# Summing the squares of two rmsnorms: running total on VectorE, or a matmul per row block on TensorE

## The chip, the cores and the metric

The kernel runs on one core of a Trainium2 chip, as one program. The metric is the device time of one execution in microseconds (us). Before the change the median of three timed runs is 3715.22 us (3713.12 to 3716.41).

## The reference

The reference is one decoder layer for a 512-token prompt and 8 decode tokens together (520 columns in the kernel). What matters here are two of its rmsnorms: `h2 = rmsnorm(x, g_ffn)` after the output projection, and the final `rmsnorm(xp, g_final)`.

```python
def rmsnorm(x, g):
    y = xf * lax.rsqrt(jnp.mean(xf * xf, axis=-1, keepdims=True) + EPS) * g
...
    x = x + mix @ lp['w_out']
    h2 = rmsnorm(x, lp['g_ffn'])
    x = x + peer(h2, ...)
...
y_prompt = rmsnorm(xp, g_final)
```

The mean runs over the 2048 model channels of a token, so each norm needs, per token, the sum of 2048 squares.

## The kernel before

The activations lie channel-first: `xt` is 128 partitions x 16 blocks (`KT`) x 520 tokens. One block `xt[:, k, :]` holds 128 channels of all tokens. A sum over channels is therefore a sum over 16 blocks and then over 128 partitions. The sum over partitions is a matmul with a 128x128 matrix of ones, in f32, in two column halves of 264 and 256 (`HALVES`), because a PSUM bank takes 512 columns.

The program has five stages with a barrier of all engines between them: `stage_a` (input projection), `stage_m` (attention and state space), `stage_d` (GLU and output projection), `stage_e` (PEER scores and the expert inputs), `stage_f` (the expert outputs and the final norm). Each engine runs its own instructions in the order in which they are written and is tied to the others by semaphores. Nothing is scheduled by a planner.

All weights come as 324 units of 1 MB. Each goes through SP's queue (DMA to `raw`), ScalarE (`split_hi`, the rounded upper part `wh`), GpSimd (`split_lo`, the rest `wl`), and then TensorE, with three fp32r matmuls per tile (`wh` with the upper and the lower part of the moving data, `wl` with the upper part). Two buffers alternate.

In `stage_d` the output projection has 16 units of 96 matmuls, one unit for each block of `xt`. The first has a loop of its own (L1204 to L1206), the others go through `unit_matmuls` (L138 to L140). After a unit, VectorE adds the result to `xt` (L1270), ScalarE squares that block into one of two slots of `sq` (L1158) and stores it, and VectorE adds the square to a running total (L1276). After the last unit TensorE multiplies the total by the ones (L1215). The next stage begins with a square root of the result (L1357).

In `stage_f` a group (`g`, 32 of them) has four units (`n`), and a unit has four tiles (`d`) of 12 matmuls (L1806 to L1808). Each tile belongs to one block of `xt`, and VectorE adds it there (L1878). Only in the last group do the blocks become final. From its second unit on ScalarE squares them (`square`, L1764), four to a unit, into four slots of `sq`. VectorE adds them to a total in `rs` (`add_square`, L1848 and L1851), two after each tile of the units 2 and 3. Then come the matmul with ones (L1822), the square root (L1789), the reciprocal (L1890) and 16 multiplications (L1894), each followed by its store.

ScalarE's order in the last group is: the split of the weights for unit 3, which waits for the tiles of unit 1, and only behind it the squares 0 to 3.

Of the kernel before, what the change touches and what calls it, by code (L numbers as in the profile page):

```python
# [12 lines left out]
ALU = mybir.AluOpType  # L13
# [6 lines left out]
KT = D // P  # L20
NS, NT = 8, 512
T = NS + NT
HALVES = ((0, 264), (264, 256))
H = 8
# [1058 lines left out]
def stage_d(nc, m, ins, outs):  # L1083

    at, sem = m.at, m.sem
# [3 lines left out]
    sq = at("sq2", [P, 4, T]); stg = at("stg", [P, 2, 2, T]); rs = at("head_rs", [H, T]); bgl = at("bgl", [P, 8]); gsub = at("gsub", [P, 2])  # L1089
    to_row = at("to_row", [P, H, H]); from_row = at("from_row", [H, H, P])  # L1090
    gh, gl = m.gh, m.gl
    total = sq[:, 2, :]
    S = {n: sem("d_" + n) for n in "const_in x_in row_ready head_squared head_summed head_root root_inverse head_spread head_scaled gain_ready heads_hi heads_lo glu_tile glu_kept sigmoid_ready mixed mixed_hi mixed_lo squares_ready squares_added residual_added".split()}
    with nc.Block() as block:
        @block.sync
        def _(sp):
# [25 lines left out]
        @block.scalar  # L1122
        def _(act):
            act.wait_ge(S["const_in"], 32)
            for n in range(N_GLU):
                u = U_GLU + n
                for j, (t, hf) in enumerate(GLU_TILES):
                    act.wait_ge(S["glu_tile"], 4 * n + j + 1)
                    if n >= 2 and hf == 0:
                        act.wait_ge(S["mixed"], 2 * (n - 2) + t + 1)  # L1130
                    c0, w = HALVES[hf]
                    act.activation(stg[:, n % 2, t, c0:c0 + w], m.acc[:, t, hf, 0:w], ACT.Sigmoid, bias=bgl[:, 2 * n + t:2 * n + t + 1]).then_inc(S["glu_kept"], 1)
                if n == N_GLU - 1:
                    act.wait_ge(S["glu_kept"], 4 * N_GLU)
                    act.sem_inc(m.acc_free, N_GLU)
                split_hi(m, act, u + 2, n % 2, (u + 2) // 2)
                if n == 0:
                    act.wait_ge(S["head_summed"], H)
                    for hf, (c0, w) in enumerate(HALVES):
                        act.activation(rs[:, c0:c0 + w], m.aux[0:H, hf, 0:w], ACT.Sqrt, bias=m.eps[0:H, 0:1], scale=1.0 / P).then_inc(S["head_root"], 1)  # L1140
                if n == N_GLU - 1:
                    for h in HEADS_SPLIT[n]:
                        act.wait_ge(S["head_scaled"], 2 * h + 2)
                        act.activation(m.hh[:, h, :], ot[:, h, :], ACT.Copy).then_inc(S["heads_hi"], 1)
                for t in range(2):
                    act.wait_ge(S["mixed"], 2 * n + t + 1)
                    act.activation(m.hh[:, 8 + 2 * n + t, :], yg[:, 2 * n + t, :], ACT.Copy).then_inc(S["mixed_hi"], 1)
                if n < N_GLU - 1:
                    for h in HEADS_SPLIT[n]:
                        act.wait_ge(S["head_scaled"], 2 * h + 2)  # L1150
                        act.activation(m.hh[:, h, :], ot[:, h, :], ACT.Copy).then_inc(S["heads_hi"], 1)
            with act.Fori(0, N_OUT // 2) as i:
                for s in range(2):
                    split_hi(m, act, i * 2 + (U_OUT + s + 2), s, i + (U_OUT // 2 + 1))

                    act.wait_ge(S["residual_added"], i * 2 + (s + 1))
                    act.wait_ge(S["squares_added"], i * 2 + (s + 1))
                    act.activation(sq[:, s, :], m.xt[:, ds(i * 2 + s, 1), :].rearrange("p a n -> p (a n)"), ACT.Square).then_inc(S["squares_ready"], 1)  # L1158
                    act.dma_start(m.x2[:, ds(i * 2 + s, 1), :].rearrange("p a n -> p (a n)"), m.xt[:, ds(i * 2 + s, 1), :].rearrange("p a n -> p (a n)")).then_inc(m.x2_stored, 16)

        @block.tensor
        def _(pe):
# [43 lines left out]
                    mm = pe.matmul(o, m.wl[0][:, k, :], m.hh[:, k, c0:c0 + w], start=False, stop=(k == KT - 1))  # L1206
            mm.then_inc(m.mm_done, 1)

            unit_matmuls(m, pe, U_OUT + 1, 1, m.hh, m.hl, 1)
            with pe.Fori(0, N_OUT // 2 - 1) as i:  # L1210
                for s in range(2):
                    unit_matmuls(m, pe, i * 2 + (U_OUT + s + 2), s, m.hh, m.hl, s)
            pe.wait_ge(S["squares_added"], KT + 2)
            for h, (c0, n) in enumerate(HALVES):
                pe.matmul(m.aux[:, h, 0:n], m.ones[:, :], total[:, c0:c0 + n], start=True, stop=True)  # L1215

        @block.vector
        def _(dve):
            dve.memset(to_row[:, :, :], 0.0).then_inc(S["row_ready"], 1)
            dve.tensor_copy(from_row[:, :, :], m.ident[0:H, 0:H].unsqueeze(2).broadcast_to([H, H, P])).then_inc(S["row_ready"], 1)  # L1220
            dve.wait_ge(S["row_ready"], 2)
# [38 lines left out]
                    for h in HEADS_SPLIT[n]:  # L1260
                        head_low(h)
            dve.wait_ge(S["x_in"], 16)
            dve.wait_ge(S["head_summed"], H)
            dve.memset(total, 0.0).then_inc(S["squares_added"], 2)
            with dve.Fori(0, N_OUT // 2) as i:
                for s in range(2):
                    dve.wait_ge(m.mm_done, i * 2 + (U_OUT + s + 3))
                    for hf, (c0, n) in enumerate(HALVES):
                        x = m.xt[:, ds(i * 2 + s, 1), c0:c0 + n].rearrange("p a n -> p (a n)")
                        x = dve.tensor_tensor(x, x, m.acc[:, s, hf, 0:n], ALU.add)  # L1270
                    x.then_inc(S["residual_added"], 1)
                    dve.wait_ge(S["residual_added"], i * 2 + (s + 1))
                    dve.sem_inc(m.acc_free, 1)
                    dve.wait_ge(S["squares_ready"], i * 2 + (s + 1))
                    dve.wait_ge(S["squares_added"], i * 2 + (s + 2))
                    dve.tensor_tensor(total, total, sq[:, s, :], ALU.add).then_inc(S["squares_added"], 1)  # L1276

TK = 16
HK = H * TK
# [8 lines left out]
GRP, NG = 4, 32  # L1288
# [399 lines left out]
def stage_f(nc, m, ins, outs):  # L1688
# [10 lines left out]
    sq = at("sq3", [P, 4, T]); rs = at("rs3", [P, T])  # L1699
    vg = [at(f"vg{j}", [P, D]) for j in range(GW)]  # L1700
    y_tok = m.aux[:, :, :].rearrange("p a n -> p (a n)")
    S = {n: sem("g_" + n) for n in "x_in ain0 ain1 gin0 gin1 weighed first_weighed weighed_hi first_hi weighed_lo first_lo sum_added tile_done rows_added y_kept y_turned squares_ready squares_added squares_summed root_ready out_ready out_stored".split()}
    ain, gin = [S["ain0"], S["ain1"]], [S["gin0"], S["gin1"]]
    vg_in = [sem(f"g_vgin{j}") for j in range(GW)]
    with nc.Block() as block:
# [42 lines left out]
        def _(act):  # L1748
# [10 lines left out]

            def square(k):  # L1760
                if k >= 4:
                    act.wait_ge(S["squares_added"], k - 3)
                act.wait_ge(S["sum_added"], 4 + 16 * (NG - 1) + k + 1)
                act.activation(sq[:, k % 4, :], m.xt[:, k, :], ACT.Square).then_inc(S["squares_ready"], 1)  # L1764

# [18 lines left out]
            turn(NG // 2 - 1, True)  # L1784
            for k in range(KT - 4, KT):
                square(k)
            act.wait_ge(S["squares_summed"], 1)
            for h, (c0, n) in enumerate(HALVES):
                act.activation(rs[:, c0:c0 + n], m.aux[:, h, 0:n], ACT.Sqrt, bias=m.eps[:, 0:1], scale=1.0 / D).then_inc(S["root_ready"], 1)  # L1789

        @block.tensor
        def _(pe):
            def turn(i, last):
                for gg in range(2):
                    g = i * 2 + gg
                    pe.wait_ge(S["weighed_lo"], g + 1)
                    for n in range(4):
# [12 lines left out]
                        if last and gg == 0 and n == 3:  # L1810
                            pe.wait_ge(S["y_kept"], 1)
                            for k in range(KT):
                                mm = pe.transpose(m.aux[:, k // 4, P * (k % 4):P * (k % 4) + P], y_sb[:, P * k:P * k + P], m.ident[:, :])
                                if k % 4 == 3:
                                    mm.then_inc(S["y_turned"], 1)

            with pe.Fori(0, NG // 2 - 1) as i:
                turn(i, False)
            turn(NG // 2 - 1, True)
            pe.wait_ge(S["squares_added"], KT)  # L1820
            for h, (c0, n) in enumerate(HALVES):
                mm = pe.matmul(m.aux[:, h, 0:n], m.ones[:, :], rs[:, c0:c0 + n], start=True, stop=True)  # L1822
            mm.then_inc(S["squares_summed"], 1)

        @block.vector
        def _(dve):
# [11 lines left out]
            def add_row(k):  # L1838
# [3 lines left out]
                else:  # L1842
                    dve.wait_ge(S["rows_added"], k)
                    dve.scalar_tensor_tensor(y_tok, vg[k % GW][:, :], m.w0[:, k:k + 1], y_tok, ALU.mult, ALU.add).then_inc(S["rows_added"], 1)  # L1844
            def add_square(k):
                dve.wait_ge(S["squares_ready"], k + 1)
                if k == 0:
                    dve.tensor_copy(rs[:, :], sq[:, 0, :]).then_inc(S["squares_added"], 1)  # L1848
                else:
                    dve.wait_ge(S["squares_added"], k)  # L1850
                    dve.tensor_tensor(rs[:, :], rs[:, :], sq[:, k % 4, :], ALU.add).then_inc(S["squares_added"], 1)  # L1851

            dve.wait_ge(ain[0], 16)
            dve.wait_ge(gin[0], 16)
            for e in range(GRP):
# [10 lines left out]
            for g in range(NG):  # L1866
                for n in range(4):
# [6 lines left out]
                    for d in range(4):  # L1874
# [4 lines left out]
                        if d == 1:  # L1879
                            for k in range(sums_by(j), sums_by(j + 1)):  # L1880
                                add_row(k)
                        if g == NG - 1 and n >= 2:
                            for k in range(8 * n + 2 * d - 16, min(8 * n + 2 * d - 14, KT)):
                                add_square(k)
                    if n == 1 and g + 1 < NG:
                        weigh(g + 1)
                    if n == 2 and g + 1 < NG:
# [2 lines left out]
            dve.reciprocal(rs[:, :], rs[:, :]).then_inc(S["tile_done"], 1)  # L1890
            dve.wait_ge(S["tile_done"], 16 * NG + 1)
            for k in range(KT):
                dve.wait_ge(S["squares_summed"], 1)
                dve.scalar_tensor_tensor(m.xt[:, k, :], m.xt[:, k, :], m.gains[:, 2, k:k + 1], rs[:, :], ALU.mult, ALU.mult).then_inc(S["out_ready"], 1)  # L1894


# [105 lines left out]
```

## Time and profile before

| | |
|---|---|
| timed runs, median | 3715.22 us |
| the profiled execution's own time | 3715.22 us |
| its span in the trace | 3713.4 us |
| TensorE busy | 3500.0 us (94%) |
| VectorE busy | 2172.1 us (58%) |
| ScalarE busy | 1066.3 us (29%) |
| GpSimd busy | 1911.3 us (51%) |
| mean granted TensorE clock | 0.978 |

The span is what the trace covers, and the rest of the execution (1.8 us) lies around it. PE is TensorE, PEld its weight loads, DVE VectorE, ACT ScalarE, POOL GpSimd. A matmul's row in the trace is longer than the distance to the next one, because matmuls overlap: throughput is read from the distance between starts. One f32 matmul appears as two rows, so a pair of them over both halves is "x4".

### The profile page before, as it was taken

The page shows a single profiled execution, that of the slowest core. Times are in us where ns is not written, and L with a number is a line of the kernel's source. Part 1 is how long each engine was busy: PE and PEld are TensorE (multiplying, and loading weights), DVE is VectorE, ACT ScalarE, POOL GpSimd, SP SyncE. Part 2 cuts the span into 40 slices and gives each one's busy share as a digit, 9 for nine tenths or more (in the row PEclk, how much of TensorE's full clock was granted, in tenths as well). Part 3 has the DMA queues.
Part 4 walks back from the last instruction along what each step waited for, and adds up shares of the span by engine and source line. Part 5 has one row for each costly group of instructions (what it writes and reads, how often), then busy time and mean ns, then how long its engine had stood idle before and what let it go on. Part 6 is the DMA issues. An engine that isn't in the chain of part 4 may idle for free. (4 is left out here: it accounts for less than half of the span.)

```text
span 3713.4 us, 57544 instructions
## 1 busy us (share of the span) xinstructions
PE 3500.0 (94%) x22728; PEld 3311.5 (89%) x22728; DVE 2172.1 (58%) x3937; ACT 1066.3 (29%) x1164; POOL 1911.3 (51%) x725
## 2 busy tenths in 40 slices
PE   8999987789998999999999999997999999999997
PEld 7978854447997999999999999997999999999997
DVE  6843224225444999964454444543677777777775
ACT  4111132243223232333333333332222222222222
POOL 3423206002334445665666666654766676767673
PEclk9999989999998999999999999998999999999998
DMA  4497978572322235767777677767778878778783
GB/s 158 159 356 296 356 275 301 180 238 108 123 101 81 79 113 194 285 264 273 274 294 278 266 279 297 280 267 275 298 278 301 298 286 301 288 296 301 291 295 129
DMA packets 257541, 910.77 MB, mean 245 GB/s; under 512 B 98353, under 2 KB 131634, under 8 KB 179378
## 3 DMA queue, kind: packets, MB, share of 16 engines
q1 hardware_dynamic: 170642, 558.22, 42.2%
q0 software_dynamic: 36864, 268.45, 17.5%
q10 hardware_dynamic: 49888, 82.24, 6.3%
q8 instruction: 81, 1.33, 0.1%
q14 instruction: 66, 0.54, 0.0%
HBM read 828.34 MB, written 78.12 MB: 244 GB/s over the span
## 5 line engine op out<-in xcount | busy, mean ns | idle before, releaser
L123 POOL TENSOR_TENSOR wl<-raw,wh 128x2048 fp32r<-128x2048 f32 x322 | 1515.8, 4708 | 1378.4 <-ACT wh L119 1378.4
L119 ACT ACTIVATE wh<-raw 128x2048 fp32r<-128x2048 f32 x324 | 620.4, 1915 | 2061.9 <-PE acc L1477 713.2
L1806 PE MATMUL acc<-vh,wh 128*128 128x392 f32 x2048 | 703.5, 344 | 42.1 <-DVE xt L1878 21.3
L1475 PE MATMUL acc<-hh,wh 128*128 128x392 f32 x2048 | 709.8, 347 | 7.1 <-POOL wl L123 7.1
L1476 PE MATMUL acc<-hl,wh 128*128 128x392 f32 x2048 | 698.5, 341 | 0.0
L1807 PE MATMUL acc<-vl,wh 128*128 128x392 f32 x2048 | 696.7, 340 | 0.0
L1477 PE MATMUL acc<-hh,wl 128*128 128x392 f32 x2048 | 696.0, 340 | 0.0
L1808 PE MATMUL acc<-vh,wl 128*128 128x392 f32 x2048 | 695.7, 340 | 0.0
L138 PE MATMUL acc<-hh,wh 128*128 128x256 f32 (+1 forms) x1952 | 555.8, 285 | 12.7 <-POOL wl L123 6.2
L139 PE MATMUL acc<-hl,wh 128*128 128x256 f32 (+1 forms) x1952 | 553.0, 283 | 0.0
L140 PE MATMUL acc<-hh,wl 128*128 128x256 f32 (+1 forms) x1952 | 551.4, 282 | 0.0
L1631 DVE SCALAR_TENSOR_TENSOR ug<-ug,aux 128x2048 f32<-128x2048 f32 x128 | 292.6, 2287 | 301.6 <-DMA ug<-expert_u,idx 300.9
L1806 PEld LDWEIGHTS acc<-vh,wh 128*128 128x128 f32 x2048 | 385.2, 188 | 53.2 <-DVE xt L1878 31.4
L1878 DVE TENSOR_TENSOR xt<-xt,acc 128x392 f32<-128x392 f32 x512 | 274.7, 557 | 220.6 <-PE acc L1808 214.2
L138 PEld LDWEIGHTS acc<-hh,wh 128*128 128x128 f32 x1952 | 369.3, 189 | 29.8 <-issue 19.0
L1475 PEld LDWEIGHTS acc<-hh,wh 128*128 128x128 f32 x2048 | 385.2, 188 | 7.4 <-ACT ast L1401 7.4
L1476 PEld LDWEIGHTS acc<-hl,wh 128*128 128x128 f32 x2048 | 385.4, 188 | 0.0
L1808 PEld LDWEIGHTS acc<-vh,wl 128*128 128x128 f32 x2048 | 385.3, 188 | 0.0
L1807 PEld LDWEIGHTS acc<-vl,wh 128*128 128x128 f32 x2048 | 385.3, 188 | 0.0
L1477 PEld LDWEIGHTS acc<-hh,wl 128*128 128x128 f32 x2048 | 385.2, 188 | 0.0
L139 PEld LDWEIGHTS acc<-hl,wh 128*128 128x128 f32 x1952 | 369.2, 189 | 0.0
L140 PEld LDWEIGHTS acc<-hh,wl 128*128 128x128 f32 x1952 | 369.0, 189 | 0.0
(335 smaller groups left out, 3954.1 us busy)
## 6 DMA issues: line engine op xcount, KB each, us to landing
raw<-units SPq DMA_DIRECT2D x324, 1024.0 KB, 4.8
kr<-cache_k SPq DMA_DIRECT2D x128, 512.0 KB, 6.8
vr<-cache_v SPq DMA_DIRECT2D x128, 512.0 KB, 6.2
expert_acts<-ast ACTq DMA_DIRECT2D x128, 196.0 KB
expert_gates<-gs ACTq DMA_DIRECT2D x14, 1792.0 KB, 6.3
a<-expert_acts SPq DMA_DIRECT2D x32, 784.0 KB
g<-expert_gates SPq DMA_DIRECT2D x32, 784.0 KB
output_steps<-qo ACTq DMA_DIRECT2D x16, 288.0 KB, 8.2
```

The source lines that it names most:

```text
L119: act.activation(m.wh[s][:, :, :], m.raw[s][:, :, :], ACT.Copy).then_inc(m.hi_done, 1)
L123: pool.tensor_tensor(m.wl[s][:, :, :], m.raw[s][:, :, :], m.wh[s][:, :, :].bitcast(F32), ALU.subtract).then_inc(m.lo_done, 1)
L138: pe.matmul(o, m.wh[s][:, k, :], rhs_hi[:, k, c0:c0 + n], start=(k == k_range[0]), stop=False)
L139: pe.matmul(o, m.wh[s][:, k, :], rhs_lo[:, k, c0:c0 + n], start=False, stop=False)
L140: mm = pe.matmul(o, m.wl[s][:, k, :], rhs_hi[:, k, c0:c0 + n], start=False, stop=(k == k_range[-1]))
L1475: pe.matmul(o, m.wh[s][:, k, :], m.hh[:, k, NA:T], start=(k == 0), stop=False)
L1476: pe.matmul(o, m.wh[s][:, k, :], m.hl[:, k, NA:T], start=False, stop=False)
L1477: mm = pe.matmul(o, m.wl[s][:, k, :], m.hh[:, k, NA:T], start=False, stop=(k == KT - 1))
L1631: dve.scalar_tensor_tensor(ug[k % GW][:, :], ug[k % GW][:, :], 1.0, m.aux[:, :, :].rearrange("p a n -> p (a n)"), ALU.mult, ALU.mult, accu ...
L1806: pe.matmul(o, m.wh[s][:, 4 * e + d, :], vh[gg][:, e, :], start=(e == 0), stop=False)
L1807: pe.matmul(o, m.wh[s][:, 4 * e + d, :], vl[gg][:, e, :], start=False, stop=False)
L1808: mm = pe.matmul(o, m.wl[s][:, 4 * e + d, :], vh[gg][:, e, :], start=False, stop=(e == GRP - 1))
```

## The change

In both stages the running total on VectorE is taken out. TensorE multiplies each block's square by the ones itself and lets PSUM accumulate over the 16 blocks (`start` at the first, `stop` at the last). The semaphore `squares_added`, which freed a slot of `sq` for ScalarE, becomes `squares_summed`, raised by TensorE after each pair.

```diff
 (stage_d, ScalarE)
-                    act.wait_ge(S["squares_added"], i * 2 + (s + 1))
+                    act.wait_ge(S["squares_summed"], i * 2 + (s + 1))
 (stage_d, TensorE)
+            def add_squares(s, count, first=False, last=False):
+
+                pe.wait_ge(S["squares_ready"], count)
+                for h, (c0, n) in enumerate(HALVES):
+                    mm = pe.matmul(m.aux[:, h, 0:n], m.ones[:, :], sq[:, s, c0:c0 + n], start=first, stop=last, skip_group_check=True)
+                mm.then_inc(S["squares_summed"], 1)
+
             unit_matmuls(m, pe, U_OUT + 1, 1, m.hh, m.hl, 1)
+            add_squares(0, 1, first=True)
             with pe.Fori(0, N_OUT // 2 - 1) as i:
                 for s in range(2):
                     unit_matmuls(m, pe, i * 2 + (U_OUT + s + 2), s, m.hh, m.hl, s)
-            pe.wait_ge(S["squares_added"], KT + 2)
-            for h, (c0, n) in enumerate(HALVES):
-                pe.matmul(m.aux[:, h, 0:n], m.ones[:, :], total[:, c0:c0 + n], start=True, stop=True)
+                    add_squares(1 - s, i * 2 + (s + 2))
+            add_squares(1, KT, last=True)
 (stage_d, VectorE)
+            dve.sem_inc(S["squares_summed"], 2)
-            dve.wait_ge(S["head_summed"], H)
-            dve.memset(total, 0.0).then_inc(S["squares_added"], 2)
-                    dve.wait_ge(S["squares_ready"], i * 2 + (s + 1))
-                    dve.wait_ge(S["squares_added"], i * 2 + (s + 2))
-                    dve.tensor_tensor(total, total, sq[:, s, :], ALU.add).then_inc(S["squares_added"], 1)
 (stage_f, ScalarE)
                 if k >= 4:
-                    act.wait_ge(S["squares_added"], k - 3)
+                    act.wait_ge(S["squares_summed"], k - 3)
-            act.wait_ge(S["squares_summed"], 1)
+            act.wait_ge(S["squares_summed"], KT)
 (stage_f, TensorE)
+            def add_squares(k):
+                pe.wait_ge(S["squares_ready"], k + 1)
+                for h, (c0, n) in enumerate(HALVES):
+                    mm = pe.matmul(m.aux[:, h, 0:n], m.ones[:, :], sq[:, k % 4, c0:c0 + n], start=(k == 0), stop=(k == KT - 1), skip_group_check=True)
+                mm.then_inc(S["squares_summed"], 1)
...
+                        if last and gg == 1 and n >= 1:
+                            for k in range(4 * n - 4, 4 * n):
+                                add_squares(k)
...
-            pe.wait_ge(S["squares_added"], KT)
-            for h, (c0, n) in enumerate(HALVES):
-                mm = pe.matmul(m.aux[:, h, 0:n], m.ones[:, :], rs[:, c0:c0 + n], start=True, stop=True)
-            mm.then_inc(S["squares_summed"], 1)
+            for k in range(KT - 4, KT):
+                add_squares(k)
 (stage_f, VectorE)
-            def add_square(k):
-                dve.wait_ge(S["squares_ready"], k + 1)
-                if k == 0:
-                    dve.tensor_copy(rs[:, :], sq[:, 0, :]).then_inc(S["squares_added"], 1)
-                else:
-                    dve.wait_ge(S["squares_added"], k)
-                    dve.tensor_tensor(rs[:, :], rs[:, :], sq[:, k % 4, :], ALU.add).then_inc(S["squares_added"], 1)
-
-                        if g == NG - 1 and n >= 2:
-                            for k in range(8 * n + 2 * d - 16, min(8 * n + 2 * d - 14, KT)):
-                                add_square(k)
```

TensorE's instructions at the end of the output projection before (`wh_64` is a weight buffer, `stg` belongs to the next stage, the branches close the loop and the stage):

```order
L139 MATMUL acc<-hl,wh_64 128x256
L140 MATMUL acc<-hh,wl_66 128x256
L1210 REGISTER_ALU
L1210 COMPARE_AND_BRANCH
L1215 MATMUL aux<-sq_12094,ones 128x264
L1215 MATMUL aux<-sq_12094,ones 128x256
L1094 UNCONDITIONAL_BRANCH
```

And the same place after. The pair of L1212 in front of the loop's branch stands behind each odd unit, and a like pair behind each even one:

```order
L139 MATMUL acc<-hl,wh_64 128x256
L140 MATMUL acc<-hh,wl_66 128x256
L1210 REGISTER_ALU
L1212 MATMUL aux<-sq_12094,ones 128x264
L1212 MATMUL aux<-sq_12094,ones 128x256
L1217 REGISTER_ALU
L1217 COMPARE_AND_BRANCH
L1212 MATMUL aux<-sq_12094,ones 128x264
L1212 MATMUL aux<-sq_12094,ones 128x256
L1093 UNCONDITIONAL_BRANCH
```

Fourteen pairs now stand in the stream between two units of the projection, one follows its last unit, and a last one closes the sum. Before there was one pair, behind everything.

TensorE's instructions in the last group of `stage_f`, where unit 2 passes to unit 3, after (before, no instruction stood between the two):

```order
L1815 MATMUL acc<-vl_20703,wh_63 128x392
L1816 MATMUL acc<-vh_20701,wl_65 128x392
L1798 MATMUL aux<-sq_20705,ones 128x264
L1798 MATMUL aux<-sq_20705,ones 128x256
L1798 MATMUL aux<-sq_20705,ones 128x264
L1798 MATMUL aux<-sq_20705,ones 128x256
L1798 MATMUL aux<-sq_20705,ones 128x264
L1798 MATMUL aux<-sq_20705,ones 128x256
L1798 MATMUL aux<-sq_20705,ones 128x264
L1798 MATMUL aux<-sq_20705,ones 128x256
L1814 MATMUL acc<-vh_20701,wh_64 128x392
L1815 MATMUL acc<-vl_20703,wh_64 128x392
```

Four pairs stand behind unit 1, four behind unit 2 and eight behind unit 3. Before, one pair stood behind unit 3.

VectorE's instructions at the end of that group before:

```order
L1878 TENSOR_TENSOR xt<-xt,acc 128x392 x9
L1848 COPY rs_20702<-sq_20701 128x520
L1851 TENSOR_TENSOR rs_20702<-rs_20702,sq_20701 128x520
L1878 TENSOR_TENSOR xt<-xt,acc 128x392
L1851 TENSOR_TENSOR rs_20702<-rs_20702,sq_20701 128x520 x2
L1878 TENSOR_TENSOR xt<-xt,acc 128x392
```

and after:

```order
L1879 TENSOR_TENSOR xt<-xt,acc 128x392 x16
L1888 RECIPROCAL rs_20706<-rs_20706 128x520
L1892 SCALAR_TENSOR_TENSOR xt<-xt,gains,rs_20706 128x520 x16
```

VectorE now has only the 16 additions of tiles there, with nothing between them.

## Rows read from the trace of the kernel before

**Rows 1.** The page, part 1: busy time, share of the span, instructions of each engine

```profile
PE 3500.0 (94%) x22728; PEld 3311.5 (89%) x22728; DVE 2172.1 (58%) x3937; ACT 1066.3 (29%) x1164; POOL 1911.3 (51%) x725
```

**Rows 2.** Busy time by engine in stretches (clock, DMA share, GB/s last)

```profile
925.00:1110.00 185.00, 179.95 (x1493) 179.74 (x1491) 84.74 (x50) 39.06 (x32) 72.26 (x16) 0.99 0.32 120
...
3654.00:3674.00 20.00, 20.00 (x115) 20.00 (x114) 6.51 (x13) 5.03 (x5) 9.80 (x3) 1.00 0.20 72
```

**Rows 3.** Who waited for whom, 925 to 1110 us (total, times, longest)

```profile
ACT wh L119 <- PE acc L140: 135.6, 15, 9.0
POOL wl L123 <- ACT wh L119: 114.6, 16, 11.6
DVE xt L1270 <- PE acc L140: 66.3, 15, 4.4
```

**Rows 4.** VectorE's timeline, first and last unit of the projection (start, length)

```profile
932.91 0.76 DVE L1270 TENSOR_TENSOR xt<-xt,acc 128x264 f32 x2 [2.52 <-PE acc L1206]
...
1105.09 0.76 DVE L1270 TENSOR_TENSOR xt<-xt,acc 128x264 f32 x2 [4.42 <-PE acc L140]
1107.54 4.48 DVE L1276 TENSOR_TENSOR sq<-sq 128x520 f32<-128x520 f32 x1 [1.69 <-ACT sq L1158]
```

**Rows 5.** TensorE's timeline in the first stage, around one pair with ones

```profile
21.48 0.29 PE L353 MATMUL acc<-hh,wl 128*128 128x256 f32 x1
21.61 1.04 PE L358 MATMUL aux<-sq,ones 128*128 128x264 f32 x4
22.29 0.47 PE L351 MATMUL acc<-hh,wh 128*128 128x264 f32 x1
22.60 0.29 PE L352 MATMUL acc<-hl,wh 128*128 128x264 f32 x1
```

**Rows 6.** TensorE's timeline in the GLU, around one pair with an 8-row matrix

```profile
900.34 0.28 PE L1188 MATMUL acc<-gh,wl 128*128 128x256 f32 x1
900.55 1.14 PE L1174 MATMUL aux<-head_rs,from_row 8*128 8x264 f32 x4
901.62 0.39 PE L1186 MATMUL acc<-gh,wh 128*128 128x264 f32 x1
901.84 0.28 PE L1187 MATMUL acc<-gl,wh 128*128 128x264 f32 x1
```

**Rows 7.** Timelines of TensorE, ScalarE and GpSimd at the end of `stage_d`

```profile
1104.67 0.28 PE L140 MATMUL acc<-hh,wl 128*128 128x256 f32 x1
1112.08 2.10 PE L1215 MATMUL aux<-sq,ones 128*128 128x264 f32 x4 [7.13 <-DVE sq L1276]
...
1106.80 0.62 ACT L1158 ACTIVATE sq<-xt 128x520 f32 x1
1114.99 1.28 ACT L1357 ACT_TABLE_LOAD   x1 [7.56 <-PEq L1920]
...
1106.97 4.50 POOL L123 TENSOR_TENSOR wl<-raw,wh 128x2048 fp32r<-128x2048 f32 x1 [6.85 <-ACT wh L119]
```

**Rows 8.** ScalarE's timeline in the last group and behind it

```profile
3671.43 1.92 ACT L119 ACTIVATE wh<-raw 128x2048 fp32r<-128x2048 f32 x1 [6.62 <-PE acc L1808]
3673.25 2.20 ACT L1764 ACTIVATE sq<-xt 128x520 f32<-128x520 f32 x4
...
3694.06 0.84 ACT L1789 ACTIVATE rs<-aux,eps 128x264 f32<-128x264 f32 x2 [1.09 <-PE aux L1822]
```

**Rows 9.** TensorE's timeline, the start of unit 2 and the end of unit 3

```profile
3671.17 0.34 PE L1806 MATMUL acc<-vh,wh 128*128 128x392 f32 x1
...
3688.06 0.34 PE L1808 MATMUL acc<-vh,wl 128*128 128x392 f32 x1
3692.45 1.57 PE L1822 MATMUL aux<-rs,ones 128*128 128x264 f32 x4 [4.05 <-DVE rs L1851]
```

**Rows 10.** TensorE after a short idle time, and the clock behind it

```profile
923.77 0.39 PE L1204 MATMUL acc<-hh,wh 128*128 128x264 f32 x1 [2.67 <-DVE hl L1243]
```

**Rows 11.** Busy time by engine in the stretch behind that idle time

```profile
924.00:929.00 5.00, 5.00 (x31) 5.00 (x30) 1.55 (x3) 0.00 (x0) 0.00 (x0) 0.66 0.87 374
```

More of the change, by code:

```diff
@@ L1091, in stage_d @@
     gh, gl = m.gh, m.gl
-    total = sq[:, 2, :]
-    S = {n: sem("d_" + n) for n in "const_in x_in row_ready head_squared head_summed head_root root_inverse head_spread head_scaled gain_ready heads_hi heads_lo glu_tile glu_kept sigmoid_ready mixed mixed_hi mixed_lo squares_ready squares_added residual_added".split()}
+    S = {n: sem("d_" + n) for n in "const_in x_in row_ready head_squared head_summed head_root root_inverse head_spread head_scaled gain_ready heads_hi heads_lo glu_tile glu_kept sigmoid_ready mixed mixed_hi mixed_lo squares_ready squares_summed residual_added".split()}
     with nc.Block() as block:
@@ L1701, in stage_f @@
     y_tok = m.aux[:, :, :].rearrange("p a n -> p (a n)")
-    S = {n: sem("g_" + n) for n in "x_in ain0 ain1 gin0 gin1 weighed first_weighed weighed_hi first_hi weighed_lo first_lo sum_added tile_done rows_added y_kept y_turned squares_ready squares_added squares_summed root_ready out_ready out_stored".split()}
+    S = {n: sem("g_" + n) for n in "x_in ain0 ain1 gin0 gin1 weighed first_weighed weighed_hi first_hi weighed_lo first_lo sum_added tile_done rows_added y_kept y_turned squares_ready squares_summed root_ready out_ready out_stored".split()}
     ain, gin = [S["ain0"], S["ain1"]], [S["gin0"], S["gin1"]]
@@ L1892, in _ @@
             for k in range(KT):
-                dve.wait_ge(S["squares_summed"], 1)
+                dve.wait_ge(S["squares_summed"], KT)
                 dve.scalar_tensor_tensor(m.xt[:, k, :], m.xt[:, k, :], m.gains[:, 2, k:k + 1], rs[:, :], ALU.mult, ALU.mult).then_inc(S["out_ready"], 1)
```

## The prediction

> **What bounds the kernel now.** I read four views: the page's busy times, the stretches of the two stages that the diff touches, the waits there, and then the timelines. The page shows TensorE busy for 94% of the span [rows 1]. An average says little about one stage, so the stretches come next. In the output projection (925 to 1110 us) TensorE works 180 of 185 us at clock 0.99, and in the last group of the expert outputs 20.0 of 20.0 us [rows 2]. The waits of the projection say the same from the other side: ScalarE waits 135.6 us and VectorE 66.3 us for matmuls, GpSimd 114.6 us for ScalarE's split, and no row has TensorE waiting [rows 3]. VectorE's first addition of a unit starts at 932.91 us and the sixteenth at 1105.09 us [rows 4]. That is 11.48 us per unit, or 0.120 us for each of its 96 matmuls. The unit's period is TensorE's own work and nothing else.
>
> VectorE's addition of a square lies inside these 11.48 us. It may take 4.48 us, since it ends before the next unit's result arrives. So inside the loops the change takes work from an engine that has time and gives it to the one that has none. Only at the ends of the two stages, where TensorE waits for VectorE's total, can it gain.
>
> **Price of a pair.** The first stage already does what the change does, on the same matrix of ones, with the same halves, between fp32r matmuls. From the last fp32r matmul ahead of a pair (21.48 us) to the second behind it (22.60 us) pass 1.12 us [rows 5]. Without the pair these would be two steps of 0.12 us. The pair costs 1.12 - 0.24 = 0.88 us. The second pair in this program that stands between fp32r matmuls has a matrix of 8 rows: 900.34 to 901.84 us is 1.50, less 0.24 is 1.26 us [rows 6]. I take 0.88, because shape and operand are those of the change, and keep 1.26 as the upper end. The same rows give a lower end: the next matmul starts 0.68 us after the pair (22.29 - 21.61), less one step is 0.56 us.
>
> **Output projection.** Unit 0 is followed by no pair. Units 1 to 14 are each followed by one, with the square of the block before, which ScalarE finished long ago (at 1107.4 us for a unit that ended at 1104.9, with 11.5 us of time). None waits. 14 x 0.88 = 12.3 us, all on the path. ScalarE's slot is freed by the pair one unit earlier, so it doesn't wait either. The weights have two buffers and all their engines wait for TensorE [rows 3]: longer units only give them more time.
>
> **The end of the projection.** The last fp32r matmul ends at 1104.67 + 0.28 = 1104.95 us, the last square at 1107.42, VectorE's addition at 1112.02, and the pair at 1112.08 + 2.10 = 1114.18. ScalarE begins the next stage at 1114.99, 0.81 us later [rows 4, 7]. Now the pair of block 14 runs 1104.95 to 1105.8, and that of block 15 starts behind the square, at 1107.5, and ends about 1108.5 (1.04 us long, rows 5). This would be 5.7 us earlier. But what is late next is GpSimd's split of a weight unit for the next stage, 1106.97 + 4.50 = 1111.47 us [rows 7], and the barrier waits for all engines. The stage ends at 1111.47 + 0.81 = 1112.3: a gain of 2.7 us, with 0 and 5.7 as bounds.
>
> That gain rests on the split not becoming shorter. VectorE's addition starts 0.57 us after the split and takes 4.48 us, where its data are those of a tile addition of 0.76 us [rows 4, 7]: it ends 0.55 us after the split does, so it is VectorE that was held up. The Trainium skill ("SBUF — State Buffer", section "Who interferes with whom") says that a VectorE instruction with two SBUF inputs and a GpSimd instruction that reads SBUF exclude each other, and that the one that started first keeps the ports. By that rule GpSimd lost nothing here and gains nothing, and the 2.7 us stand; were it GpSimd that was slowed, the gain would go towards 5.7 us.
>
> **The last group of the expert outputs.** Behind unit 1 TensorE meets the pairs of blocks 0 to 3. Before, unit 2 began right there, at 3671.17 us [rows 9]. But ScalarE writes these squares only behind its split for unit 3, which itself waits for unit 1: split at 3671.43 for 1.92 us, squares from 3673.25, the first ready after 0.62 (as in rows 7), at 3673.9 [rows 8]. This is the wait that the change adds. TensorE stands 2.7 us, then runs four pairs, 3.5 us. ScalarE writes a square each 0.5 us (four in 2.20), faster than the pairs take them. Queued behind are the tiles of unit 2, and VectorE behind them. Delay: 6.2 us.
>
> Behind unit 2 four pairs, 3.5 us. Their squares wait only for pairs 0 to 3 and are ready. The tiles' end moves from 3688.06 + 0.34 = 3688.4 [rows 9] to 3688.4 + 6.2 + 3.5 = 3698.1 us. Then come eight pairs, 7.0 us, to 3705.1. The square of block 15 has to wait for pair 11 (3701.6 us) and is ready at 3702.3, before pair 15 at 3704.3, so ScalarE doesn't stretch these. The square root starts at once, as it did before (3694.06, with the pair at 3692.45 + 1.57) [rows 8, 9]. 3705.1 against 3694.06 is +11.1 us. The reciprocal, the multiplications and stores behind it don't change. VectorE's fifteen additions and one copy vanish, and with them the 4.05 us that TensorE waited before its one pair [rows 9]; this gain is already in the difference.
>
> **Sum.** 12.3 - 2.7 + 11.1 = +20.7 us. The profiled execution took 3715.22 us (span 3713.4 and 1.8 around it), which is also the median of the timed runs. Forecast 3736 us, 0.56% slower.
>
> **Rivals.**
>
> *The clock falls behind the new wait.* After an idle time of 2.67 us TensorE ran on at full clock from 923.77 us, but in the 5 us from 924 to 929 its mean clock was 0.66 [rows 10, 11]: part of them was at 1.2 instead of 2.4 GHz, and 5 x 0.34 = 1.7 us of work were lost. The new wait is as long. Against it: TensorE waited 2.67 us here and the fall came a microsecond after it had resumed, so it isn't certain for each such wait. The time would be 3737.6 us. The Trainium skill ("TensorE: Matmul & The Clock Gate", section "What's actually happening") calls the slow clock the default that activity releases; by that rule the price is due wherever activity has been low, and the trace shows it once for a wait like this.
>
> *A pair costs 1.26 us.* For: rows 6 are from the same stage, a few units earlier. Against: an 8-row matrix. The 14 pairs of the projection cost 5.3 us more. In the last group only the first of a run of pairs follows an fp32r matmul, three times, 1.1 us more. Sum 27.1, 3742.3 us.
>
> *A pair costs 0.56 us.* 30 pairs, 14 in the projection and 16 in the last group, 0.32 us less each: 9.6 us less, 3726 us.
>
> *The pairs hide (the other side).* If TensorE took the f32 pairs beside its stream, as an engine that really is at 94% busy and not full might, the projection keeps its 11.48 us. Its end gains 2.7 us. In the last group the 2.7 us wait remains, and the tiles end at 3691.1; then block 15 is added (0.6), squared (0.6) and summed (1.0), 3693.3, which is 0.8 us earlier than before. In all -3.5 us, 3712 us, no measurable change. It decides from a price of a pair below about 0.25 us. Against it: the stretch of rows 2 has no idle time in it, and rows 5 show the price.
>
> **How the numbers follow.** A difference of 0.2% (7.4 us) is about what a measurement of this kernel can tell. The forecast's mechanism at 0.88 us a pair has 0.82, of it 0.25 with the fallen clock. 1.26 us a pair has 0.09, 0.56 us a pair 0.05, hidden pairs 0.04. Around the likeliest, 0 to 5.7 us at the projection's end and the clock give 3733 to 3739. Half-way to the two other prices of a pair, the range is 3730 to 3741. Slower by over 0.2% (above 3722.7 us) are all cases but the hidden pairs: 0.95. Within 0.2%: 0.04. Faster: 0.01.
>
> **What would show it right or wrong.** The distance between VectorE's additions to `xt` in the projection should be 12.36 us instead of 11.48. The last stretch of the projection should have GpSimd's split as the last to end, with ScalarE's table load 0.8 us behind it. In the last group TensorE should show one idle row of about 2.6 us ended by ScalarE's square, at the first pair, and eight pairs in a row at the end, with the square root 7 us behind the start of VectorE's last tile addition. I am wrong if the unit's period stays near 11.5 us, if ScalarE's squares 12 to 15 wait so long that TensorE idles between pairs, or if the next stages' times move by more than a microsecond or two.

## The result and the profile after

The changed kernel takes 3741.47 us (median of four executions, 3737.15 to 3747.69) against 3714.63 us. The ratio is 1.0073, with a 95% interval of 1.0056 to 1.0088: slower, as forecast, but 0.5 us above the top of the stated range. Two more executions of it, one of them the profiled one, took 3739.66 and 3737.37 us, which makes the median of all six 3739.88 us. A second set gave 3738.39 us (six executions, 3736.50 to 3751.59) against 3716.02 us, ratio 1.0069 (1.0053 to 1.0085). The profiled execution's span is 3735.6 us.

The page after, part 1 [answers rows 1]:

```profile
PE 3527.1 (94%) x22848; PEld 3333.5 (89%) x22848; DVE 2076.8 (56%) x3904; ACT 1066.8 (29%) x1164; POOL 1912.3 (51%) x725
```

VectorE lost 95 us of busy time and TensorE gained 27. The engine that was relieved was not the bound.

The projection on VectorE's timeline, the first two and the last unit [answers rows 4]:

```profile
931.36 0.76 DVE L1275 TENSOR_TENSOR xt<-xt,acc 128x264 f32 x2 [5.82 <-PE acc L1205]
942.83 0.76 DVE L1275 TENSOR_TENSOR xt<-xt,acc 128x264 f32 x2 [10.71 <-PE acc L140]
955.19 0.76 DVE L1275 TENSOR_TENSOR xt<-xt,acc 128x264 f32 x2 [11.60 <-PE acc L140]
...
1115.87 0.76 DVE L1275 TENSOR_TENSOR xt<-xt,acc 128x264 f32 x2 [11.60 <-PE acc L140]
```

The first distance is still 11.47 us, for no pair follows unit 0. The fourteen others are (1115.87 - 942.83) / 14 = 12.36 us. From the first addition to the last pass 184.51 us, before 172.18: +12.33 us.

TensorE, ScalarE and GpSimd at the end of that stage [answers rows 7]:

```profile
1115.57 1.04 PE L1212 MATMUL aux<-sq,ones 128*128 128x264 f32 x4
1118.25 1.14 PE L1212 MATMUL aux<-sq,ones 128*128 128x264 f32 x4 [1.65 <-ACT sq L1157]
...
1117.58 0.62 ACT L1157 ACTIVATE sq<-xt 128x520 f32 x1
1123.12 1.28 ACT L1359 ACT_TABLE_LOAD   x1 [4.92 <-PEq L1918]
...
1117.75 4.50 POOL L123 TENSOR_TENSOR wl<-raw,wh 128x2048 fp32r<-128x2048 f32 x1 [7.74 <-ACT wh L119]
```

TensorE ends at 1119.39 us. GpSimd ends at 1122.25, and the next stage begins 0.87 us behind it. From VectorE's last addition to the table load it is 7.25 us, before 9.90: -2.65 us. The split takes 4.50 us as before, though VectorE's addition no longer runs beside it. So TensorE's last two pairs cost the projection nothing: they end 2.86 us before GpSimd does.

The last group, ScalarE and then TensorE [answers rows 8 and 9]. The first two lines are VectorE's addition of the last tile of unit 1, before and after:

```profile
3671.37 0.56 DVE L1878 TENSOR_TENSOR xt<-xt,acc 128x392 f32<-128x392 f32 x1 [1.57 <-PE acc L1808]
3680.58 0.56 DVE L1879 TENSOR_TENSOR xt<-xt,acc 128x392 f32<-128x392 f32 x1 [1.57 <-PE acc L1816]
...
3680.64 1.91 ACT L119 ACTIVATE wh<-raw 128x2048 fp32r<-128x2048 f32 x1 [6.62 <-PE acc L1816]
3682.45 2.20 ACT L1766 ACTIVATE sq<-xt 128x520 f32<-128x520 f32 x4
...
3716.23 0.85 ACT L1791 ACTIVATE rs<-aux,eps 128x264 f32<-128x264 f32 x2 [1.57 <-PE aux L1798]
...
3683.13 5.46 PE L1798 MATMUL aux<-sq,ones 128*128 128x264 f32 x16 [2.59 <-ACT sq L1766]
...
3696.97 3.67 PE L1798 MATMUL aux<-sq,ones 128*128 128x264 f32 x16
3709.02 7.17 PE L1798 MATMUL aux<-sq,ones 128*128 128x264 f32 x32
```

The wait at the first pair is there, 2.59 us, ended by ScalarE's square. Behind unit 2 four pairs take 3.67 us from the first start to the last end. The same four behind unit 1 take 5.46. The clock says why:

```profile
3683.10:3688.10 5.00, 4.97 (x15) 3.99 (x16) 0.00 (x0) 3.18 (x6) 4.04 (x1) 0.66 0.00 0
```

The last but two of these numbers is the mean granted clock, 0.66 of 2.4 GHz, so part of the five microseconds ran at 1.2 GHz. It is the picture of rows 11. From VectorE's addition of the last tile of unit 1 (3680.58 us, before 3671.37) to the square root (3716.23, before 3694.06) it is 35.65 us instead of 22.69: +12.96 us. That is 11.1 us from the sum and about 1.8 us for the clock (5.46 - 3.67 = 1.79 us for the first four pairs).

So the two profiled executions differ by 12.33 - 2.65 + 12.96 = +22.64 us in the changed stretches. Whole they differ by 22.15 us; the remaining -0.5 us lies in the untouched stretches: the first addition of the projection came 1.55 us earlier, the stretch from the next stage's table load to the last group took 1.1 us longer.

The 1.55 us are worth a look, for they are the clock again. TensorE's wait of 2.67 us at the head of the projection, that of rows 10, is still there after the change, but no fall of the clock follows it. TensorE after that wait, and the same five microseconds as in rows 11:

```profile
923.76 0.39 PE L1203 MATMUL acc<-hh,wh 128*128 128x264 f32 x1 [2.67 <-DVE hl L1250]
...
924.00:929.00 5.00, 5.00 (x43) 5.00 (x43) 1.54 (x3) 0.00 (x0) 0.00 (x0) 1.00 0.89 381
```

From that matmul to the first addition it is 7.60 us, before 9.14. TensorE's instructions in this stretch are the same before and after.

### The profile page after: what moved, and what is told of

Its sections match the earlier page's. It is cut to its first block and busy times, and to the rows that moved or that the text cites. A ratio compares the mean times of both kernels' runs of the same rounds, so it can differ in the third digit from the quotient of the medians.

```text
span 3735.6 us, 57742 instructions
## 1 busy us (share of the span) xinstructions
PE 3527.1 (94%) x22848; PEld 3333.5 (89%) x22848; DVE 2076.8 (56%) x3904; ACT 1066.8 (29%) x1164; POOL 1912.3 (51%) x725
```

## The experiments

**Each half alone.** The first kernel takes the change only in the output projection, the second only in the last group, and the third is the changed kernel once more on the same chip.

```diff
 (projection alone: stage_d of the changed kernel, the rest of the kernel before)
 (last group alone: stage_f of the changed kernel, the rest of the kernel before)
```

> The change in the output projection alone (the last group as before). Theory 1, that the time is the sum of the pieces read in the traces: 14 pairs at 0.88 us on the path, less 2.7 us at the stage's end, +9.6 us over the kernel before, 3724 us, and executions as close together as those of the kernel before (within 4 us). Theory 2, that the 4 us by which the median lies above the profiled execution come with the projection (shifted waits of the stages behind it): +14 us and a spread of 10 us.

Measured: 3724.88 us (12 executions), ratio 1.0021 (1.0010 to 1.0032), +8.9 us. In the trace the projection took 184.51 us from first to last addition and 7.25 us to the next stage, exactly as in the changed kernel. Theory 1 holds for the time. Its second half, that executions lie within 4 us, fell: they went from 3718.88 to 3732.24 us. But so did the kernel before beside it, 22 executions from 3708.37 to 3727.99 us. The spread is there without the change.

> The change in the last group alone (the projection as before). Theory 1, the sum of the pieces: 2.7 us of waiting, 16 pairs of 0.88 us, less the 4 us that TensorE waited for VectorE's total and its own slow pair: +11.1 us, and +12.8 where the clock falls behind the wait, so 3726 to 3728 us, in two heaps 1.7 us apart. Theory 2, that the excess comes with the last group: +15 us or more, with the spread of 10 us.

Measured: 3726.61 us (11 executions), ratio 1.0030 (1.0021 to 1.0040), +10.6 us. TensorE's wait and its pairs in that kernel's last group:

```profile
3674.48 5.18 PE L1796 MATMUL aux<-sq,ones 128*128 128x264 f32 x16 [2.59 <-ACT sq L1764]
...
3688.05 3.67 PE L1796 MATMUL aux<-sq,ones 128*128 128x264 f32 x16
3700.09 7.17 PE L1796 MATMUL aux<-sq,ones 128*128 128x264 f32 x32
```

The same wait, and again a slower first run of pairs: the clock was 0.71 from 3674.5 to 3679.5 us. From unit 1's end to the square root it is 35.38 us, +12.7; the median's +10.6 us is lower, with an interval of 7.8 to 14.9 us that holds both. The two heaps 1.7 us apart can't be seen in a spread of 11 us.

> The changed kernel once more, beside its two halves on the same chip, for the spread of its executions. Theory 1: the median is the sum of the two halves' differences, +20.7 to +22.4 us, 3735 to 3738 us, and the 3747.7 us seen once is a rare outlier. Theory 2, that executions of this kernel vary by 10 us: a median again near 3741 us with values up to 3747 us.

Measured: 3738.39 us, +22.4 us. The halves sum to 8.9 + 10.6 = 19.5 us, which agrees within the intervals. The median is what theory 1 said. Its rare outlier is none: 3745.85 and 3751.59 us came too. Theory 2 is right on the spread, which the kernel before has as well, and wrong on the median.

**ScalarE's order.**

```diff
+                        if last and gg == 1 and n == 1:
+                            for k in range(4):
+                                square(k)
                         if not (last and gg == 1 and n >= 2):
                             split_hi(...)
...
-                        if last and gg == 1 and n >= 1:
+                        if last and gg == 1 and n >= 2:
                             for k in range(4 * n - 4, 4 * n):
                                 square(k)
```

> The changed kernel with ScalarE's squares 0 to 3 ahead of its split for unit 3 instead of behind it. Theory 1, that TensorE's new wait is ScalarE's order: the wait at the first pair goes, 2.6 us less, and the fall of the clock behind it too, 1.7 us less where it came: 2.6 to 4.4 us under the changed kernel. The split then starts up to 0.3 us later at most, unit 3 doesn't wait. Rival, that the wait would come from the pairs themselves or the split would now be late for unit 3: no gain.

Measured: 3733.78 us (6 executions) beside 3738.39 us, -4.6 us, with intervals that overlap (1.0036 to 1.0063, and 1.0053 to 1.0085). The trace is sharper. ScalarE first, then TensorE's pairs in the order of time, and last VectorE's addition at the end of unit 1 and the square root:

```profile
3669.64 2.20 ACT L1766 ACTIVATE sq<-xt 128x520 f32<-128x520 f32 x4
3676.36 1.91 ACT L119 ACTIVATE wh<-raw 128x2048 fp32r<-128x2048 f32 x1 [4.51 <-PE acc L1819]
...
3676.10 3.67 PE L1801 MATMUL aux<-sq,ones 128*128 128x264 f32 x16
3688.14 3.67 PE L1801 MATMUL aux<-sq,ones 128*128 128x264 f32 x16
3700.19 7.17 PE L1801 MATMUL aux<-sq,ones 128*128 128x264 f32 x32
...
3676.30 0.56 DVE L1882 TENSOR_TENSOR xt<-xt,acc 128x392 f32<-128x392 f32 x1 [1.57 <-PE acc L1819]
3707.40 0.85 ACT L1794 ACTIVATE rs<-aux,eps 128x264 f32<-128x264 f32 x2 [1.57 <-PE aux L1801]
```

No wait, and the first four pairs take 3.67 us like the others. The clock behind them stayed full:

```profile
3676.20:3681.20 5.00, 5.00 (x26) 4.53 (x25) 0.56 (x1) 4.09 (x5) 2.86 (x1) 1.00 0.00 0
```

From the end of unit 1 to the square root it is 31.10 us instead of 35.65, so the wait of 2.59 us and the clock's 1.8 us both went. The Trainium skill ("TensorE: Matmul & The Clock Gate", section "What's actually happening") says that the slow clock is the default and that activity releases it. The trace of the last group agrees: 1.00 where TensorE worked on, 0.66 behind the wait.

In this place the fall goes with the wait. It came in each of the six traces whose last group has the wait (the changed kernel twice, the last group alone, and three kernels below), with 0.66 to 0.71 over the five microseconds from the first pair on, and in none of the four without. But a wait of this length isn't always followed by a fall. TensorE's wait of 2.65 to 2.67 us at the head of the projection stands in all ten traces, and the clock fell behind it in three: those of the kernel before, of this one and of the kernel with fp32r pairs below. There the first addition came 9.14 to 9.16 us behind the matmul that ended the wait, in the other seven 7.60 to 7.62. Why the two places differ was not tried.

**What a pair costs.** Two kernels, one with the pairs in fp32r in place of f32, and one with 8 of the 128 rows (it leaves out the other 120 rows of each square in the projection).

```diff
 (fp32r, both stages: onesr a copy of the ones, sqr and sq3 buffers of fp32r)
-  pe.matmul(m.aux[:, h, 0:n], m.ones[:, :], sq[:, s, c0:c0 + n], ...)
+  pe.matmul(m.aux[:, h, 0:n], onesr[:, :], sqr[:, s, c0:c0 + n], ...)
 (eight rows, projection only)
-  pe.matmul(m.aux[:, h, 0:n], m.ones[:, :], sq[:, s, c0:c0 + n], ...)
+  pe.matmul(m.aux[:, h, 0:n], m.ones[0:8, :], sq[0:8, s, c0:c0 + n], ...)
```

> The changed kernel with the squares written and multiplied as fp32r (less precise than f32), in buffers of that type. Theory 1, that the price of a pair is its matmuls' columns, four times as long in f32: a pair costs 2 x 0.12 = 0.24 us, the projection's period is 11.72 us, its end still gains 2.6 us, +0.7 us there; in the last group the wait of 2.6 us stays, the pairs follow ScalarE's squares at 0.5 us each, and its end comes 3.0 us later than before, 4.8 where the clock falls: +4 to +5.5 us over the kernel before, some 17 us under the changed one. Rival, that a pair costs because it breaks the stream (another kind of matmul, another semaphore): 0.6 us or more stays of it, +14 us or more.

Measured: 3721.60 us (11 executions), ratio 1.0016 (1.0008 to 1.0025), +6.2 us, somewhat above the 4 to 5.5 us expected. First and last addition of the projection, and the last group's pairs:

```profile
927.54 0.76 DVE L1277 TENSOR_TENSOR xt<-xt,acc 128x264 f32 x2 [7.38 <-PE acc L1207]
1103.24 0.76 DVE L1277 TENSOR_TENSOR xt<-xt,acc 128x264 f32 x2 [10.97 <-PE acc L140]
...
3670.40 2.38 PE L1802 MATMUL aux<-sq,ones_r 128*128 128x264 f32 x8 [2.59 <-ACT sq L1770]
3681.75 1.12 PE L1802 MATMUL aux<-sq,ones_r 128*128 128x264 f32 x8
3691.24 3.22 PE L1802 MATMUL aux<-sq,ones_r 128*128 128x264 f32 x16
```

175.70 us, 3.52 more than before, are 0.25 us a pair. From unit 1's end to the square root it is +4.7 us (4.8 expected, with the clock). So 0.63 of the 0.88 us come with f32 in place of fp32r. The 0.25 us left are two steps of 0.12, which leaves nothing for breaking the stream.

> The changed kernel with each pair of the projection over 8 of the 128 rows (it leaves out 120 of 128 rows of each square there). Theory 1, that the pair in the GLU cost 1.26 us by its 8-row matrix: the projection's period grows from 12.36 to 12.74 us. Rival, that it cost this by its place (a tile's end, its semaphores): the period stays 12.36 us.

Measured: 3748.03 us (one execution). The first and the last addition of the projection are 189.92 us apart.

```profile
938.46 0.76 DVE L1275 TENSOR_TENSOR xt<-xt,acc 128x264 f32 x2 [5.83 <-PE acc L1205]
1128.38 0.76 DVE L1275 TENSOR_TENSOR xt<-xt,acc 128x264 f32 x2 [11.99 <-PE acc L140]
```

(189.92 - 172.18) / 14 = 1.27 us a pair. With 8 rows instead of 128 a pair is dearer, and by as much as rows 6 had it. So that rival price came with the operand's shape and not with the place.

**What ends the projection.**

```diff
-                    split_hi(m, act, i * 2 + (U_OUT + s + 2), s, i + (U_OUT // 2 + 1))
                     act.wait_ge(S["residual_added"], i * 2 + (s + 1))
                     ... square, store ...
+                    split_hi(m, act, i * 2 + (U_OUT + s + 2), s, i + (U_OUT // 2 + 1))
```

> The changed kernel with ScalarE squaring a block of the projection ahead of splitting the next weights. It makes TensorE's last pair earlier and GpSimd's last split later. Theory 1, that the stage now ends with GpSimd's split: from the last addition to xt to the next stage's table load 8.7 us instead of 7.25. Rival, that it ends with TensorE: 5.7 us.

Measured: 3738.26 us (one execution). VectorE, TensorE, GpSimd and ScalarE:

```profile
1116.12 0.76 DVE L1274 TENSOR_TENSOR xt<-xt,acc 128x264 f32 x2 [11.60 <-PE acc L140]
...
1117.69 1.14 PE L1211 MATMUL aux<-sq,ones 128*128 128x264 f32 x4 [0.84 <-ACT sq L1155]
...
1119.54 4.49 POOL L123 TENSOR_TENSOR wl<-raw,wh 128x2048 fp32r<-128x2048 f32 x1 [7.67 <-ACT wh L119]
...
1124.90 1.28 ACT L1358 ACT_TABLE_LOAD   x1 [5.43 <-PEq L1917]
```

TensorE ended at 1118.83 us, 2.7 us behind the last addition where it was 3.5 in the changed kernel, and still the stage ended later: 8.78 us from the last addition (8.7 expected), 0.87 us behind GpSimd's end (1124.03). The stage ends with GpSimd's split.

**The gains without the pairs in the loops.** The running total stays on VectorE; only the last blocks are left to TensorE, where it has nothing else to do.

```diff
 (stage_d, TensorE, behind the loop; VectorE leaves out the addition of block 15)
-            pe.wait_ge(S["squares_added"], KT + 2)
+            pe.wait_ge(S["squares_added"], KT + 1)
             (pair on total, start)
+            pe.wait_ge(S["squares_ready"], KT)
+            (pair on sq[:, 1, :], stop)
 (stage_f: ScalarE as in the kernel with early squares; TensorE behind the group)
+            (pair on the square of block 14, pair on that of block 15, pair on rs)
 (stage_f, VectorE)
+ADDED_BEHIND = {(1, 0): (0,), (1, 1): (1,), ... (2, 3): (7,), (3, 0): (8, 9), (3, 1): (10, 11), (3, 2): (12,), (3, 3): (13,)}
```

> The kernel before with VectorE's running total kept, but without its last additions: in the projection it totals blocks 0 to 14, and TensorE, idle at the end anyway, takes one pair on the total and one on the square of block 15; in the last group VectorE totals blocks 0 to 13, one addition behind each tile from unit 1 on, TensorE takes three pairs (total, 14, 15), and ScalarE squares blocks 0 to 3 ahead of its split for unit 3. Theory 1, that a pair costs only where TensorE has no gap, and that the gains at the two ends are real: no pair stands in a loop, the projection's period stays 11.48 us, its end comes 2.6 us earlier (GpSimd's split is then last), the last group's 2.7 us: -5.3 us, about 3711 us. Rival, that the gain at the ends hangs on the pairs inside the loops: no gain, 3716 us.

Measured: 3711.78 us (12 executions) against 3715.45 us, ratio 0.9993 (0.9984 to 1.0003). The median moved the right way by 3.7 us, but the interval holds no change: the times alone do not show a gain. The trace shows one at both ends:

```profile
927.83 0.76 DVE L1272 TENSOR_TENSOR xt<-xt,acc 128x264 f32 x2 [1.18 <-PE acc L1206]
1099.91 0.76 DVE L1272 TENSOR_TENSOR xt<-xt,acc 128x264 f32<-128x264 f32 x2 [4.31 <-PE acc L140]
...
1107.25 1.28 ACT L1365 ACT_TABLE_LOAD   x1 [4.91 <-PEq L1939]
...
3681.97 0.56 DVE L1897 TENSOR_TENSOR xt<-xt,acc 128x392 f32<-128x392 f32 x1 [0.96 <-PE acc L1821]
...
3685.37 0.84 ACT L1802 ACTIVATE rs<-aux,eps 128x264 f32<-128x264 f32 x2 [0.81 <-PE aux L1835]
```

The projection keeps its 172.08 us and its end takes 7.34 us instead of 9.90. In the last group the square root comes 3.4 us behind the end of TensorE's last tile (3681.93 us, where VectorE's addition starts); before, it came 5.7 us behind it (3688.40 to 3694.06) [rows 8, 9]. Together about -4.8 us where 5.3 were expected. It has the lowest median of all versions run, and its gain is at the edge of what can be measured.

## Why the prediction was wrong, point by point

- *The bound is TensorE in both stretches.* Right. None of TensorE's new work inside the loops was hidden.
- *A pair costs 0.88 us* [rows 5]. Right to the hundredth: 12.33 us over 14 pairs. The rivals at 1.26, at 0.56 and hidden are refuted, and the eight rows explain the 1.26.
- *The projection's end gains 2.7 us, and GpSimd's split is late next.* Right: 2.65 us, and the kernel that squares first confirms what ends the stage.
- *ScalarE's split holds up the first square and TensorE stands 2.7 us.* Right: 2.59 us, gone when the squares go first.
- *The last group costs 11.1 us.* This is the step of the sum that failed: it measured +12.96 us. Its waits and pairs were right: with the squares early it is 31.10 us, and 31.10 + 2.59 - 22.69 = 11.0. What it put at nothing was the fall of the clock behind the new wait, +1.8 us. I held that for a rival, with 0.25 of 0.82, on the ground that the fall isn't certain for each such wait. As a general statement this holds: behind the wait of rows 10 the clock fell in three of ten traces. In the last group it fell in six of six. With the term the sum is 12.3 - 2.7 + 12.9 = 22.5 us and the forecast 3738 us. The second set's +22.4 us and the 22.64 us of the changed stretches say the same.
- *The range from 3730 to 3741 us.* This failed too. It was built from the costs of the mechanism alone and has no term for how the median of a few executions scatters, though the prediction itself says that 0.2% (7.4 us) is about what a measurement can tell. The three executions of the kernel before lay within 3.3 us; 22 and 23 of them run from 3708.4 to 3728.0 and from 3711.6 to 3723.4 us. Medians of four drawn at random from those 22 scatter by 2.5 us (one standard deviation, an estimate from these times).

So the mechanism stands and a term was missing, but the missing term does not by itself bring the time out of the range. The pieces over the first set's own base give 3714.63 + 22.64 = 3737.3 us, and 3741.47 us lies 4.2 us above it. The profiled execution of that set took 3737.37 us; no trace shows its slower ones, and what made them slower stays open. The second set doesn't repeat them (3716.02 + 22.64 = 3738.7 us, its median 0.3 below), and the first set's six executions together have 3739.88 us, inside the range. That the median of four fell 0.5 us outside is in part chance.

What makes the executions of one kernel differ is only partly settled. In 103 executions of eight sets (each taken against its own set's mean, the first set left out) the time goes with the mean granted clock, with a correlation of -0.81 and 2.4 us for each 0.001. In the traces, the falls of the clock in the untouched stages come at other places and in other lengths each time; the head of the projection is one, worth 1.55 us. That the clock alone makes the spread was not shown: in which waits the difference begins was not tried.

## What to carry to other kernels

Moving a sum from an engine with slack to the one that is full costs its full price in the loop, even when the same move gains at the stage's end; take the gain at the end alone, by giving TensorE only the last terms, for which it would wait anyway. Where a change puts a new wait ahead of the busiest engine, look at what stands ahead of its releaser on that engine's own queue: here one split of weights written in front of four squares cost 2.6 us and the clock another 1.8. Give the clock a term of its own wherever such a wait is new, for it may fall or not. And take the spread of a kernel from many executions before stating how wide the range is.

## What the runs showed of the hardware

- An f32 pair over 264 and 256 columns costs 0.88 us between fp32r matmuls with 128 rows, 1.27 us with 8 rows, and the same pair in fp32r 0.25 us. Fewer rows cost more here, not less.
- A wait of 2.6 us on TensorE was followed by a stretch at 1.2 GHz in all six traces that had it in the last group. In the five of them with f32 pairs the first four pairs took 5.18 to 5.46 us instead of 3.67, up to 1.8 us more, which is 70% of the wait itself. A wait of 2.65 to 2.67 us at the head of the projection was followed by one in three of ten traces, at a cost of 1.55 us.
- VectorE's addition of a square, two inputs of 128x520, took 4.48 us where it started behind GpSimd's split in the projection [rows 4], and 0.70 us in the last group of the same trace. In the kernel with the last blocks on TensorE one such addition took 4.62 us and its neighbours 0.69. GpSimd's last split of the projection took 4.50 us with the addition beside it and 4.50 us without, the others 4.61 to 4.62 us in both kernels.
